# The value projection of a gated recurrence: from a plain product of eight weight blocks to Strassen's seven products, with the weight sums added by transfers

## The reference, cut to what matters

```python
x = x + 0.5 * rmsnorm(swiglu(rmsnorm(x, g1), w_ffn1_in, w_ffn1_out), g1_post)
h = rmsnorm(x, mix_pre_norm)
z = h @ w_in
qa, ka, va, qh, fz_f, fz_b, ih, gh, gate_a, gate_h = split(z)
y_a = attention(qa, ka, va, rel_bias)            # three dilated head groups
v = ih                                           # 512 tokens x 1024, the values
y_h = gated_recurrence(silu(qh), gates(fz_f), gates(fz_b), v, gh)
y = sigmoid(gate_a) * (y_a @ w_proj_attn) + sigmoid(gate_h) * (y_h @ w_proj_hgrn)
x = x + rmsnorm(y @ w_out, mix_post_norm)
x = x + 0.5 * rmsnorm(swiglu(rmsnorm(x, g3), w_ffn2_in, w_ffn2_out), g3_post)
```

## Time and profile before

| | |
|---|---|
| median of three runs | 1451.23 us (1450.93 to 1547.62) |
| the profiled execution's own time | 1450.56 us |
| its span in the trace | 1448.7 us |
| TensorE busy | 1439.1 us (99% of the span) |
| VectorE busy | 867.0 us (60%) |
| ScalarE busy | 657.3 us (45%) |
| GpSimd busy | 24.4 us (2%) |
| transfers | 150.54 MB, 104 GB/s on average |

### The profile page before, as it was taken

One profiled execution on the slowest core, in us unless ns is written; L12 is line 12 of the kernel. 1 busy time (PEld: TensorE's weight loads), 2 busy tenths in 40 slices (PEclk: granted clock), 3 DMA queues, 4 the chain that ended last, 5 costly groups with the idle time before them and its releaser, 6 DMA issues.

```text
span 1448.7 us, 21247 instructions
## 1 busy us (share of the span) xinstructions
PE 1439.1 (99%) x8128; PEld 1231.9 (85%) x8128; DVE 867.0 (60%) x1381; ACT 657.3 (45%) x1066; POOL 24.4 (2%) x43
## 2 busy tenths in 40 slices
PE   9999999999999999999999999999999999999998
PEld 7799999888898888888888888888889888888886
DVE  6888775435753455454257775764447555564875
ACT  5455555334532546553244654453345333232542
POOL 0000000000100000000000000000000000000000
PEclk9999999999999999999999999999999999999999
DMA  6332323424332323222332222223331243233753
GB/s 197 117 117 93 112 88 117 130 88 131 95 109 88 91 74 89 62 73 87 102 88 73 73 71 74 72 73 117 112 106 34 98 145 101 88 100 110 242 185 131
DMA packets 43451, 150.54 MB, mean 104 GB/s; under 512 B 5191, under 2 KB 5191, under 8 KB 43376
## 3 DMA queue, kind: packets, MB, share of 16 engines
q1 hardware_dynamic: 40608, 140.53, 30.2%
q0 software_dynamic: 2624, 8.95, 2.0%
q10 hardware_dynamic: 144, 0.04, 0.0%
HBM read 144.49 MB, written 4.23 MB: 103 GB/s over the span
## 4 chain that ended last, share of the span: by engine, by line
PE 96%; DVE 2%; DMA 1%; ACT 1%; issue 0%; SPq 0%; DVEq 0%; ACTq 0%
PE ps L418 21%; PE ps L419 21%; PE ps L420 21%; PE ps L570 4%; PE ps L571 4%; PE ps L572 4%; PE ps L1618 2%; PE ps L1619 2%; PE ps L1620 2%; PE ps L2279 1%; PE ps L2015 1%; PE ps L2016 1%; PE ps L2017 1%; DMA raw<-in_wstream 1%; PE ps L2158 1%; PE ps L2157 1%
## 5 line engine op out<-in xcount | busy, mean ns | idle before, releaser
L418 PE MATMUL ps<-hh,whi 128*128 128x512 f32 x976 | 386.2, 396 | 1.7 <-DVE wlo L381 1.0
L381 DVE TENSOR_TENSOR wlo<-raw,whi 128x1024 fp32r<-128x1024 f32 x180 | 220.3, 1224 | 277.0 <-ACT whi L376 276.9
L420 PE MATMUL ps<-hh,wlo 128*128 128x512 f32 x976 | 380.2, 390 | 0.0
L419 PE MATMUL ps<-hl,whi 128*128 128x512 f32 x976 | 380.2, 390 | 0.0
L376 ACT ACTIVATE whi<-raw 128x1024 fp32r<-128x1024 f32 x180 | 190.3, 1057 | 415.1 <-PE ps L420 358.2
L418 PEld LDWEIGHTS ps<-hh,whi 128*128 128x128 f32 x976 | 183.2, 188 | 46.2 <-issue 5.4
L420 PEld LDWEIGHTS ps<-hh,wlo 128*128 128x128 f32 x976 | 183.2, 188 | 38.6
L419 PEld LDWEIGHTS ps<-hl,whi 128*128 128x128 f32 x976 | 183.3, 188 | 36.4 <-issue 0.2
L418 PE MATMUL ps<-ah,whi 128*128 128x512 f32 (+1 forms) x192 | 71.7, 373 | 0.7 <-DVE wlo L381 0.7
L419 PE MATMUL ps<-al,whi 128*128 128x512 f32 (+1 forms) x192 | 71.3, 371 | 0.0
L420 PE MATMUL ps<-ah,wlo 128*128 128x512 f32 (+1 forms) x192 | 71.3, 371 | 0.0
(11 more groups left out here) (528 smaller groups left out, 2920.9 us busy)
## 6 DMA issues: line engine op xcount, KB each, us to landing
raw<-in_wstream SPq DMA_DIRECT2D x198, 512.0 KB, 3.5
w_raw<-in_wstream SPq DMA_DIRECT2D x32, 512.0 KB, 4.3
ring<-in_wstream SPq DMA_DIRECT2D x20, 512.0 KB, 4.4
xt<-in_x_t SPq DMA_DIRECT2D x16, 256.0 KB, 4.6
x_dram<-x_tok POOLq DMA_DIRECT2D x4, 512.0 KB, 4.1
x_tok<-x_dram POOLq DMA_DIRECT2D x4, 512.0 KB, 5.5
out<-out_tok SPq DMA_DIRECT2D x8, 256.0 KB, 2.0
bias<-vec_dram POOLq DMA_DIRECT2D x8, 192.0 KB, 3.3
```

The lines of the kernel that those rows point to most:

```text
L381: nc.vector.tensor_tensor(wlo[:, s, :], raw[:, s, :], whi[:, s, :].bitcast(F32), ALU.subtract).then_inc(split_done, 1)
L418: nc.tensor.matmul(out, w, m, start=start, stop=False)
L419: nc.tensor.matmul(out, w, ml, start=False, stop=False)
L420: return nc.tensor.matmul(out, wl, m, start=False, stop=stop)
```

## The change

The product of 512x1024 by 1024x1024 is cut into quadrants (early and late 256 tokens, first and second half of k, first and second half of the columns) and computed with Strassen's seven products in place of eight. Each of the seven is two blocks of 12 products of 128x128 by 128x512 (2 k tiles x 2 token tiles x 3), so 14 blocks in place of 8.

- Four sums of token quadrants (t1 to t4) are made by VectorE: `h_whole` (eight instructions, two, two and four of them in gaps of the last pair of heads, `h_in_gap`), `h_sums_early` after the last attention tail, `h_sums_late` in gate A, and their split into high and low (`h_sums_head` on ScalarE, `h_sums_tail` on VectorE, four of each).
- Six blocks use the weights as loaded. The other eight use sums of weight blocks. These sums are made in place by GpSimd's queue: eight transfers from SBUF to SBUF that add (`ih_sum`), each of 512 KB, each waiting for the one before it; the first four over the blocks loaded first (k tiles 0, 1, 4, 5), the last four over those loaded last.
- Loads go to places of their own (`raw_direct`, `raw_sum`), at most two under way at a time, in the order `IH_ORDER`: four blocks to be summed, six direct ones, four to be summed.
- `whi` and `wlo` get a third slot for this stage (`whi_ih`, `wlo_ih`).
- Outputs are joined on VectorE from PSUM and from copies by ScalarE (`ih_act`, `ih_dve`).
- The counters of later stages are shifted by what the new stage adds to them; the host puts the weight blocks into the new order.

The core of the diff:

```diff
-          ("gate_a", 6), ("ih", 4), ("hgrn", 2 * GH_HEADS + 2), ...
+          ("gate_a", 6), ("ih", 7), ("hgrn", 2 * GH_HEADS + 2), ...
+        IH_U, IH_V, IH_W, IH_Z = (0, 1), (2, 3), (6, 7), (4, 5)
+        IH_ORDER = [*range(IH_DIRECT, IH_DIRECT + 4), *range(IH_DIRECT), *range(IH_DIRECT + 4, IH_BLOCKS)]
+        def ih_split(m):
+            s = m % 3
+            return (whi[:, s, :], wlo[:, s, :]) if s < 2 else (whi_ih[:], wlo_ih[:])
+        def ih_load(sp, n):
+            m = IH_ORDER[n]
+            if m < 2:
+                sp.wait_ge(split_done, IH_0 + m - 1)
+            elif m < IH_DIRECT:
+                sp.wait_ge(sem("t_sum"), IN_T_SUM + 4)
+            elif m < IH_DIRECT + 4:
+                sp.wait_ge(sem("atl_done"), PAIRS_H)
+            else:
+                sp.wait_ge(block_done, IH_0)
+            sp.wait_ge(raw_in[n % 2], 16 * ((IH_0 + n) // 2))
+            sp.dma_start(ih_raw(m), wstream[IH_0 + n]).then_inc(raw_in[n % 2], 16)
+        def ih_pe(pe):
+            for c in range(2):
+                quadrant(3 * c, c, "b11", IH_U, True)
+                quadrant(3 * c + 1, c, "b21", IH_V, True)
+                pe.wait_ge(sem("h_low"), 2 * IN_H + 2 * c + 2)
+                quadrant(3 * c + 2, c, "t4", IH_W, True)
+            pe.wait_ge(sem("y_a"), KT)
+            for c in range(2):
+                m = IH_DIRECT + 4 * c
+                quadrant(m, c, "t1", IH_Z, True)
+                pe.wait_ge(sem("q_left"), IN_Q_LEFT + 4)
+                quadrant(m + 1, c, "t3", IH_W, True)
+                quadrant(m + 2, c, "t2", IH_U, False)
+                pe.wait_ge(sem("ih_out1"), 3)
+                quadrant(m + 3, c, "b22", IH_V, True)
+        def ih_head(act, m):
+            if m >= IH_DIRECT:
+                act.wait_ge(sem("ih_summed"), 16 * (m - IH_DIRECT + 1))
+            else:
+                act.wait_ge(*ih_landed(m))
+            if m == 2:
+                act.wait_ge(sem("t_sum"), IN_T_SUM + 4)
+            else:
+                act.wait_ge(block_done, IH_0 + m - 1 if m < 2 else IH_0 + m - 2)
+            nc.scalar.activation(ih_split(m)[0], ih_raw(m), ACT.Copy).then_inc(head_done, 1)
+        def ih_sum(pool, m):
+            c, q = divmod(m - IH_DIRECT, 4)
+            w22, w21, w11, w12 = (IH_DIRECT + 4 * c + i for i in range(4))
+            a, b = ((w22, w21), (w21, w11), (w11, w22), (w12, w11))[q]
+            for x in {0: (w22, w21), 1: (w11,), 2: (), 3: (w12,)}[q]:
+                pool.wait_ge(*ih_landed(x))
+            if m > IH_DIRECT:
+                pool.wait_ge(sem("ih_summed"), 16 * (m - IH_DIRECT))
+            pool.dma_start(ih_raw(a), ih_raw(b), accum_op=ALU.add).then_inc(sem("ih_summed"), 16)
+        def ih_dve(dve):
+            ih_tail(dve, 2)
+            h_sums_tail(dve, 2)
+            ih_tail(dve, 3)
+            h_sums_tail(dve, 3)
+            ih_tail(dve, 4)
+            ih_tail(dve, 5)
+            ih_tail(dve, IH_DIRECT)
+            dve.wait_ge(block_done, IH_0 + 5)
...
@@ sync
-            load_pairs(rows_1 + 5, gates + 3)
+            load_pairs(rows_1 + 5, FIRST["ih"])
+            for m in range(IH_BLOCKS):
+                ih_load(sp, m)
+            load_pairs(FIRST["hgrn"], gates + 3)
@@ gpsimd
+            for m in range(IH_DIRECT, IH_BLOCKS):
+                ih_sum(pool, m)
@@ tensor
-            ih_pe(pe, 2)
-            pe.wait_ge(sem("ih_out0"), 5)
+            ih_pe(pe)
+            pe.wait_ge(sem("q_left"), IN_Q_LEFT + 6)
```

More of the change, by code:

```diff
@@ L303, in build @@
         att_sum = rstd[:].rearrange("p (t c) -> p t c", c=P)
+        at[0] = after_ymix
+        t_ih_raw = place("t_ih_raw", [P, KT // 2, 4, WIN])
+        at[0] = after_ymix
+        t_ih_low = place("t_ih_low", [P, KT // 2, 4, WIN], F32R)
+        t_ih_high = place("t_ih_high", [P, KT // 2, 4, WIN], F32R)
+        assert at[0] == hgrn_at
+        at[0] = first_of_pair
+        h_whole = place("h_whole", [P, KT, S])
+        assert at[0] <= second_of_pair
+        at[0] = hgrn_at
+        raw_direct = place("raw_direct", [P, 4, BLK])
+        at[0] = hgrn_at + 8 * TT * D
+        raw_sum = [place("raw_sum0", [P, 4, BLK])]
+        at[0] += 4 * S
+        assert at[0] == ath_at
+        raw_sum.append(place("raw_sum1", [P, 4, BLK]))
+        at[0] = hgrn_at + 4 * TT * D
+        whi_ih = place("whi_ih", [P, BLK], F32R)
+        wlo_ih = place("wlo_ih", [P, BLK], F32R)
+        ih_p1 = [place(f"ih_p1_{i}", [P, S])[:] for i in range(2)]
+        ih_q4 = [place(f"ih_q4_{i}", [P, S])[:] for i in range(2)]
         at[0] = hgrn_at
@@ new lines, in ih_act, with leave @@
+        def ih_act(act):
+            def leave(i, into, bank):
+                nc.scalar.activation(into[i], ps[:, bank[i], :], ACT.Copy).then_inc(sem("q_left"), 1)
+            for m in range(2, IH_BLOCKS):
+                ih_head(act, m)
+                if m == 5:
+                    act.wait_ge(block_done, IH_0 + 4)
+                    for i in range(2):
+                        leave(i, ih_p1, IH_U)
+                if m == 7:
+                    act.wait_ge(block_done, IH_0 + 6)
+                    for i in range(2):
+                        leave(i, ih_q4, IH_W)
+            head(act, FIRST["hgrn"] - 1, 0)
+            act.wait_ge(block_done, IH_0 + IH_BLOCKS - 1)
+            for i in range(2):
+                leave(i, ih_u2, IH_U)
+            head(act, FIRST["hgrn"] - 1, 1)
@@ new lines, in h_whole_dve, with h_sums_early @@
+        def h_whole_dve(dve, kt):
+            nc.vector.scalar_tensor_tensor(out=h_whole[:, kt, :], in0=xt[:, kt, :], scalar=PRE2[:, kt:kt + 1], in1=rstd[:],
+                                           op0=ALU.mult, op1=ALU.mult).then_inc(sem("h_norm"), 1)
+        def h_sums_early(dve):
+            h1, h2 = h_whole[:, 0:KT // 2, :], h_whole[:, KT // 2:KT, :]
+            t1, t3 = (t_ih_raw[:, :, n, :] for n in (0, 2))
+            early, late = TOKENS
+            dve.wait_ge(sem("h_norm"), 2 * IN_H + KT)
+            nc.vector.tensor_tensor(t3, h2[:, :, late], h1[:, :, late], ALU.subtract).then_inc(sem("t_sum"), 1)
+            nc.vector.tensor_tensor(t1, h1[:, :, early], h1[:, :, late], ALU.subtract).then_inc(sem("t_sum"), 1)
@@ new lines, in h_sums_late @@
+        def h_sums_late(dve):
+            h2 = h_whole[:, KT // 2:KT, :]
+            t1, t2, t4 = (t_ih_raw[:, :, n, :] for n in (0, 1, 3))
+            early, late = TOKENS
+            dve.wait_ge(sem("t_sum"), IN_T_SUM + 2)
+            nc.vector.scalar_tensor_tensor(out=t2, in0=t1, scalar=-1.0, in1=h2[:, :, late], op0=ALU.mult,
+                                           op1=ALU.subtract).then_inc(sem("t_sum"), 1)
+            dve.wait_ge(sem("t_sum"), IN_T_SUM + 3)
+            nc.vector.scalar_tensor_tensor(out=t4, in0=t2, scalar=-1.0, in1=h2[:, :, early], op0=ALU.mult,
+                                           op1=ALU.subtract).then_inc(sem("t_sum"), 1)
@@ L2500, in a_tail, with h_in_gap @@
                                         ).then_inc(sem("atl_done"), 1)
+            def h_in_gap(hp, a, b):
+                if hp == PAIRS_H - 1:
+                    for kt in range(a, b):
+                        h_whole_dve(dve, kt)
             for b in range(6):
@@ L2560, in gate_a_act @@
                     nc.scalar.activation(ymix[:, m, :], ymix[:, m, :], ACT.Sigmoid).then_inc(sem("sig_a_done"), 1)
-                head(act, first + b // 2, b % 2)
+                if b < 2:
+                    head(act, first, b)
+                else:
+                    ih_head(act, b - 2)
+                if b > 0:
+                    h_sums_head(act, b - 1)
+            h_sums_head(act, 3)
         def gate_a_dve(dve):
@@ L2574, in gate_a_dve @@
                                             ALU.mult).then_inc(sem("y_a"), 1)
-                tail(dve, first + b // 2, b % 2)
+                if b < 2:
+                    tail(dve, first, b)
+                else:
+                    ih_tail(dve, b - 2)
+                if b == 0:
+                    h_sums_late(dve)
+                elif b < 3:
+                    h_sums_tail(dve, b - 1)
         def both(x):
```

156 lines of the change are left out of this document (127 added, 29 removed).

## The result

The changed kernel takes 1452.55 us in the median of 20 runs, the kernel before 1450.45 in as many: a ratio of 1.0015 with a 95% interval of 1.0009 to 1.0022. It is slower, by 2.1 us where 2.2 faster was forecast. Nothing of this comes near 2%; it lies inside the range and on the other side of the kernel before.

The account below looks back on a forecast made before the run. TensorE was taken to bound the kernel, busy 1439.1 of 1448.7 us. 1450.56 - 5.44 saved + 0.2 stall + 2.6 late sums = 1447.9, stated as 1448.3 us; range 1445.0 to 1461.

Parts of the forecast that it names:

- What is saved: TensorE in the changed stage: 24 products fewer at 0.2267 us each save 5.44 us, less 0.2 us of stall.
- The work before and beside it: VectorE and ScalarE before and inside the stage: token sums, heads and tails fit idle time, costing only 0.2 us of stall.
- Where the idle time would be: TensorE waits before blocks 11 to 13, through tails, heads and a GpSimd-queue transfer; none before 6 to 9; 2.6 us late.
- signs of being wrong: Waits before block 6, transfers over 7 us, a direct load landing after 685, or a hole at the recurrence's start.
- The limits of 685 and 688: Latest landing times in us of the direct loads for blocks 4 and 5, expected to land at 682 and 685.
- The step that failed: Transfer engines beside the weight loads: 16 us of loads and 10 of adds in 25 us, first four sums done at 693.5.
- The size of the free link: One adding transfer after the loads: 2.89 us fixed plus 2.6 for twice the read, 5.5 us.
- The hidden chain: Rival: adding transfers stay under 5.5 us even beside the loads, as at a copy's 4.2, giving 1445.4 us; chance 0.28.
- The long chain: Rival: each adding transfer takes 7.2 us beside and after the loads, eighth sum 13.2 us late, 1458.6 us; chance 0.20.
- Heads and tails as the bound: Rival: heads and tails can't keep up and TensorE stalls at many of the 14 blocks, 1447.9 us; chance 0.05.
- The break-even at 6.2 us for each link: Time per adding transfer in the chain of eight above which the changed kernel is slower than before: 6.2 us.

## Why the prediction was right in its mechanism and wrong in its sign

**What is saved.** Right: 168 products at 0.2267, and the run without sums lies 1450.46 - 1445.28 = 5.18 us under the kernel before, where 5.44 - 0.2 = 5.24 was the term.

**The work before and beside it.** Right. The three gaps of attention, `h_sums_early` and `h_sums_late` cost nothing that a trace shows; without the sums no wait of TensorE is left in the stage, and the tail of block 2 came 0.1 us late as forecast.

**Where the idle time would be.** Right: blocks 11 to 13, by tails, by heads, by a transfer on GpSimd's queue, and nothing in front of blocks 6 to 9. Not foreseen was the half us in front of block 1: the load of block 0 landed at 677.5, 3 us after its head could have begun, and pushed VectorE's list in gate A.

Two of the prediction's own signs of being wrong did show. Adding transfers took over 7 us from issue to landing (the first 7.7, the fifth 7.4); that belongs to the step below. And direct loads landed after 685: those for blocks 4 and 5 at 687.8 and 691.5. This one cost nothing, for the blocks began without a gap at 691.75 and 694.47. The limits of 685 and 688 were set one block too early: from the prediction's own start of block 4, 679.67 + 0.2 + 4 x 2.72, less 2.4, comes 688.3, and 691.1 for block 5.

**The step that failed** is the term "the engines of the queues have about 12 loads x 1.3 = 16 us of work and four adds x 2.6 = 10 in 25 us", from which the fourth sum was put at 693.5 and the last loads were left where they would be with nothing beside them. The add was right for engines with room (2.65 measured, 2.93 beside the loads). The load was not: 1.3 us came from a window whose packets were all of GpSimd's queue, which was moving `x_tok` out to DRAM, while the row right above it in the same group holds the price of a weight load: 0.33 of the engines at one load per 5.44 us is 1.8 us; the run without sums gives 1.65. In that run the second of the last loads and the last land at 689.4 and 693.7, where the forecast had them (689.3 and 693.5): what it missed is what the adds do to them. Up to 697.8, when the last load could leave, there were 13 new loads, the one still under way and four adds: 14 x 1.65 + 4 x 2.65 = 33.7 us of work from 661.7 on, where the trace shows 0.92 x 36.1 = 33.2. In the forecast's own terms, 12 loads x 1.65 and four adds x 2.65 are 30.4 us from 668.5 on where it had 26 in 25: they end at 698.9. The trace has the fourth sum at 697.5 and the fifth's start at 698.26, with the engines at 0.95 in between and the last of the twelve loads barely begun.

**The size of the free link** was off the other way: 5.5 forecast, 4.7 to 4.9 measured. The part beside the engine time is smaller between places in SBUF (3.25 - 1.28 = 2.0 by the copies, 4.8 - 2.65 = 2.15 by the adds) than the 2.89 of the earlier trace rows, where the transfer ended in DRAM; that the DRAM is the reason is not shown. The two errors partly cancel: the fifth sum starts 4.8 us later than forecast (698.26 against 693.5) and its link, beside the last load, lasts 8.0 us where 5.5 was forecast (2.4 more); the last three take 14.3 us in place of 16.5 (2.2 less). That is the 5.0 us between 715.5 and 720.49. The profiled stage started 0.5 us later than before, so TensorE idles 4.5 us more at its end, and 0.5 in front of block 1: 2.8 us of idle time were forecast, 7.6 came, and 5.44 were to be had.

**Rivals.** The hidden chain (1445.4) is what copies would have given, to 0.1 us; its condition, an add at a copy's price, doesn't hold. The long chain had its 7.2 us beside the loads but not after them. Heads and tails as the bound is refuted by the run without sums. The break-even at 6.2 us for each link was right: the mean from 668.56 to 720.49 is 6.5, and the kernel is slower by 2.1, where 8 x (6.5 - 6.2) would make it 2.4.

## What to carry to other kernels

Before work is moved from an idle engine to transfers, add up the engine time of all transfers in that stretch at the price that this stretch's own rows give (share of the engines times the distance between loads), and count an adding transfer as twice a copy: here 2.65 us for 512 KB (2.93 with the engines full) against 1.28 for a copy and 1.65 for a load. Where the sum fills the stretch, everything on the transfers is late together, the loads too. And place the work where the waiting is: VectorE idled in this stage, took eight sums of 1.22 us for nothing, and its version beats both kernels (1445.19).

## What the runs showed of the hardware

- An adding transfer of 512 KB inside SBUF takes 4.4 to 4.6 us from issue to landing with nothing beside it, and its issue on GpSimd 0.85 us; a plain one takes 2.8 to 3.3 and 0.53. The profile counts the same bytes for both, and 2.65 against 1.28 us of engine time.
- Transfers and loads slow each other: in the changed kernel, with the engines at 0.92, adds land in 6.6 us and loads in 5.2 and 6.0 in the median, against 4.4 for an add alone and 4.3 and 4.5 for loads without adds.
- GpSimd's float32 add over 128x1024 takes 2.40 to 3.27 us, and VectorE's subtraction of the same size, both operands in SBUF, goes from 1.22 to as much as 3.42 us beside it.
- Executions of the changed kernel spread over 5.2 us in 20, those of the version on VectorE over 0.8 in five. The chain of transfers isn't shown to be the reason: the version on GpSimd has none and spreads over 2.4 in 11.
